# Two transformer blocks with an expert layer of gathered rows: the order of the first norm's turns, of the first expert sums and of the last gathers

## The chip, the core and the metric

The kernel is one program in Bass on one core of a Trainium2 chip: TensorE (PE) for matmuls, VectorE (DVE), ScalarE (ACT), GpSimd (POOL) and SyncE (SP), each with its own instruction queue, and 16 DMA engines that all queues share. The metric is the device time of one execution in microseconds, the median of several runs; less is better.

## What is computed

Batch 1, 256 tokens, model width 1024, float32. The second block ends with the part that takes half of the time.

```python
x = first_block(...)     # HGRN2 + pooling mixer, layer norm, squared-ReLU MLP of width 4096, layer norm
# second_block:
x = x + mixer(rmsnorm(x, norm_mix_g))          # MoBA attention, spatial gating MLP, two gates
x = x + memory_cross_attention(rmsnorm(x, norm_xa_g), rmsnorm(mem, norm_mem_g), w_q, w_kv, w_o)
x = x + peer_ffn(rmsnorm(x, norm_ffn_g), w_q, subkeys, w_down, w_up)
return rmsnorm(x, final_g)

def token_chunk(xc):                            # peer_ffn, for 128 tokens
    q = (xc @ w_q).reshape(128, 8, 2, 128)
    s = einsum("thpd,hpnd->thpn", q, subkeys)   # 8 heads, two lists of 128 scores
    s1, i1 = top_k(s[:, :, 0], 16)
    s2, i2 = top_k(s[:, :, 1], 16)
    top_s, top_pos = top_k(s1[..., :, None] + s2[..., None, :], 16)   # of 256 sums
    e = take(i1[..., :, None] * 128 + i2[..., None, :], top_pos)      # 16 of 16384 experts
    g = softmax(top_s)
    a = gelu(einsum("td,thkd->thk", xc, w_down[e]))
    return einsum("thk,thkd->td", g * a, w_up[e])
```

Each token and head reads 16 rows of w_down and 16 of w_up from HBM, 268 MB in all.

## The kernel before

**Weights.** The matmuls up to the cross attention run in a split form: ScalarE makes a high part of a weight block and VectorE the rest ("w_hi", "w_lo"), and PE multiplies three of the four products. SP loads a block of 1 MB into one of four buffers as soon as PE is done with the block four before. `take` waits for the split halves, `across` (line 646) multiplies in the transposed form, `to_across` (line 810) turns rows into columns by transposes, four at a time into one PSUM bank ("batch").

**First norm.** After the block "wo", VectorE normalizes XR in two column halves and signals `ln_z` twice. PE runs the first half of block "xka" (keys of the memory), then in `turn_first` the four batches "ln1T" 0 to 3 of four transposes each, then the second half of "xka". Of each two batches VectorE scales one into LT[:, 0] (line 2313) and ScalarE the other into LT[:, 1] (line 1501); ScalarE then copies both into the high part of both_C (line 1407) and VectorE subtracts for the low part (line 1908), after which the first "up" block (lines 691 and 694) may run its half. LT has one set of buffers: the second pair waits for the first's low part. Between its two pairs ScalarE copies "xka" out to KX (line 1384).

**Expert layer.** The 16 turns `it` are head `it % 8` of tokens 0 to 127 (turns 0 to 7) and 128 to 255 (8 to 15). For each of the 16 picks of a turn POOL issues one indirect DMA (line 3006) that gathers, for each of 128 tokens, one row of 8 KB, "down" and "up" side by side, into one buffer R. Number n = 16 it + k takes a buffer from `OPENED` (free after some earlier stage) or that of gather `USED_BY[n]`, once PE has counted its sums in `up_done`; POOL issues in strict order and waits for `idx_ready` where a new index is needed. Two picks form a pair g: VectorE's `dot_rows` (line 2783) takes the dot with the token, ScalarE the gelu, VectorE's `coefs` (line 2792) the product with the softmax weight, ScalarE two diagonal matrices DIAG (line 1802), and PE's `sums` (line 1278) adds DIAG times the "up" half into two PSUM banks, four matmul instructions a pick. Each engine's order over the turns is written out by hand.

In turn 0 the first index is ready ahead of the next seven and these ahead of the last eight (`first_eight`, `second_eight`, `decode_eight`: a position in the list of sums is split into two numbers, each looked up by comparing with iota, multiplying and adding up). Turn 0 is mixed with the cross attention of tokens 128 to 255: `cross_max` (VectorE), `cross_exps` (ScalarE, line 1713), `cross_weights` (VectorE, line 2564), `cross_turn` (PE, line 1177), `cross_turned` (ScalarE), `cross_values` (PE, line 1188) and `cross_out_second` (line 1209). `warm` loads ScalarE's table for another function.

**End.** The last pick (n = 255) has no diagonal: VectorE adds coef times its "up" row to the PSUM sums into XR, in two halves (line 2960), and the final norm and three stores follow.

## Time and profile before

| | |
|---|---|
| median of 3 runs | 1291.82 us (1291.52 to 1292.28) |
| profiled execution: its own time | 1292.65 us |
| its span, first to last instruction | 1290.9 us |
| busy: PE, DVE, ACT, POOL | 1178.1, 928.0, 555.2, 298.0 us |
| DMA: moved, mean rate | 396.14 MB, 307 GB/s |
| gathers | 256, 268.45 MB, 50.3% of 16 engines' span |
| mean granted TensorE clock | 0.990 |

How to read it: an engine's busy time is summed over stages with different limits, and PE's is modelled from pipelined starts. The profile gives time by instruction group, by stretch, and as a chain of releasers followed back from the last instruction. The numbers below are from that one profiled execution.

### The profile page before, as it was taken

Reading aid. Unit: us, or ns where it says so; the run is one execution under the profiler, and the core shown is the slowest. Engines: PE = TensorE matmul, PEld = TensorE weight load, DVE = VectorE, ACT = ScalarE, POOL = GpSimd, SP = SyncE. Lnnn points to the kernel's source line nnn. Section 1 sums busy time; section 2 is a strip of 40 time slices with the busy share of each in tenths; the row PEclk is TensorE's granted clock in tenths of the full one; section 3 lists DMA queues with packets and bytes.
Section 4 is the critical chain, followed back from the end, with each engine's and each line's share of the span. In section 5 each row is a group of like instructions: output and inputs, shape, how many; then the busy total and the mean of one; then the engine's idle time right before and its main releaser. Section 6 shows DMA issues by size and latency. Waiting matters only on the chain.

```text
span 1290.9 us, 16341 instructions
## 1 busy us (share of the span) xinstructions
PE 1178.1 (91%) x5734; PEld 829.1 (64%) x5734; DVE 928.0 (72%) x1854; ACT 555.2 (43%) x1014; POOL 298.0 (23%) x261
## 2 busy tenths in 40 slices
PE   9999999999999999999999989988987877777776
PEld 9988999888888899998855544544532323332322
DVE  6886758788854785587688786777677777777655
ACT  5833655466533547656435333332332222222312
POOL 0000000000000000000244555444554444545420
PEclk9999999999999999999999999999999999999999
DMA  7544455455555653466899999999999999999996
GB/s 290 189 170 144 164 210 208 160 191 195 210 213 192 201 194 135 166 245 238 345 400 421 418 420 419 420 419 420 420 419 420 420 420 419 422 418 422 418 421 256
DMA packets 55924, 396.14 MB, mean 307 GB/s; under 512 B 6320, under 2 KB 6320, under 8 KB 8752
## 3 DMA queue, kind: packets, MB, share of 16 engines
q0 software_dynamic: 36864, 268.45, 50.3%
q1 hardware_dynamic: 17136, 119.17, 25.6%
q10 hardware_dynamic: 1856, 7.60, 1.7%
q8 instruction: 44, 0.72, 0.2%
q14 instruction: 24, 0.20, 0.0%
HBM read 394.15 MB, written 1.05 MB: 306 GB/s over the span
## 4 chain that ended last, share of the span: by engine, by line
PE 60%; DMA 30%; DVE 5%; ACT 2%; issue 2%; POOL 1%; DVEq 0%; POOLq 0%; ACTq 0%
DMA R<-experts,IDX 30%; PE ps L646 12%; PE ps L1278 10%; PE ps L774 10%; PE ps L691 9%; PE ps L694 5%; PE ps L715 3%; PE ps L728 2%; PE ps L658 2%; PE ps L1106 2%; DVE R L2783 1%; ACT DIAG L1802 1%; POOL R L3006 1%; PE ps L1156 1%; PE ps L810 1%
## 5 line engine op out<-in xcount | busy, mean ns | idle before, releaser
L1278 PE MATMUL ps<-R,DIAG 128*128 128x512 f32 x1020 | 476.0, 612 | 97.3 <-ACT DIAG L1802 96.8
L1278 PEld LDWEIGHTS ps<-R,DIAG 128*128 128x128 f32 x1020 | 187.7, 193 | 358.0 <-issue 192.2
L3006 POOL DMA_INDIRECT R<-experts,IDX x256 | 296.7, 1159 | 513.3 <-PE ps L1278 281.7
L2783 DVE CUSTOM_DVE_ANT_0 R<-R,XN 128x1024 f32<-128x1024 f32 x256 | 312.9, 1227 | 132.8 <-DMA R<-experts,IDX 130.9
L1938 DVE TENSOR_TENSOR w_lo<-raw,w_hi 128x1024 fp32r<-128x1024 f32 x192 | 227.5, 1220 | 70.8 <-ACT w_hi L1335 66.7
L1335 ACT ACTIVATE w_hi<-raw 128x1024 fp32r<-128x1024 f32 x191 | 192.9, 1052 | 69.0 <-DMA raw<-weights 67.9
L1790 ACT ACTIVATE act_d<-dots,rst 128x2 f32<-128x2 f32 (+1 forms) x130 | 38.4, 296 | 305.3 <-DVE dots L2783 305.2
L1802 ACT ACTIVATE DIAG<-con,coef 128x128 f32<-128x128 f32 x255 | 88.6, 394 | 121.3 <-DVE coef L2792 119.0
L691 PE MATMUL ps<-both_C,w_hi 128*128 128x512 f32 x384 | 134.4, 394 | 1.3 <-DVE both_C L1908 1.3
L694 PE MATMUL ps<-both_C,w_lo 128*128 128x256 f32 x384 | 107.6, 280 | 0.0
L2984 POOL TENSOR_SCALAR_AFFINE_SELECT WS<-WS 128x1024 f32<-128x1024 f32 x1 | 1.1, 1090 | 437.7 <-DMA BS<-gbs 437.7
L691 PEld LDWEIGHTS ps<-both_C,w_hi 128*128 128x128 f32 x384 | 71.9, 187 | 18.1 <-issue 1.8
L694 PEld LDWEIGHTS ps<-both_C,w_lo 128*128 128x128 f32 x384 | 72.6, 189 | 0.0
L646 PE MATMUL ps<-both_A,w_hi 128*128 128x256 f32 x384 | 69.9, 284 | 0.2 <-issue 0.2
L646 PEld LDWEIGHTS ps<-both_A,w_hi 128*128 128x128 f32 x384 | 60.1, 192 | 0.6 <-issue 0.6
L646 PE MATMUL ps<-both_C,w_hi 128*128 128x256 f32 x320 | 58.8, 284 | 0.3 <-ACT GA L1384 0.3
L646 PE MATMUL ps<-both_A,w_lo 128*128 128x256 f32 x192 | 54.3, 283 | 0.0
L646 PEld LDWEIGHTS ps<-both_C,w_hi 128*128 128x128 f32 x320 | 50.2, 192 | 1.2 <-issue 0.7
L774 PE MATMUL ps<-w_hi,HT_hi 128*128 128x512 f32 x128 | 49.8, 389 | 0.0
L774 PE MATMUL ps<-w_lo,HT_hi 128*128 128x512 f32 x128 | 49.8, 389 | 0.0
L774 PE MATMUL ps<-w_hi,HT_lo 128*128 128x512 f32 x128 | 49.8, 389 | 0.0
L646 PE MATMUL ps<-both_C,w_lo 128*128 128x256 f32 x160 | 45.3, 283 | 0.0
(431 smaller groups left out, 1767.5 us busy)
## 6 DMA issues: line engine op xcount, KB each, us to landing
raw<-weights SPq DMA_DIRECT2D x95, 1024.0 KB, 4.8
PQW<-weights SPq DMA_DIRECT2D x8, 1024.0 KB, 7.1
R<-experts,IDX POOLq DMA_INDIRECT x256
raw<-weights SPq DMA_DIRECT2D x4, 512.0 KB, 8.6
LNR<-rows ACTq DMA_DIRECT2D x2, 1024.0 KB, 4.7
early_raw<-weights SPq DMA_DIRECT2D x2, 1024.0 KB, 6.9
XQ<-weights SPq DMA_DIRECT2D x2, 1024.0 KB, 6.6
XO<-weights SPq DMA_DIRECT2D x2, 1024.0 KB, 8.7
```

Source lines behind the costliest of these rows:

```text
L646: mm = pe.matmul(dst[:, c * T:(c + 1) * T], a[:, i, c * P:(c + 1) * P], b[:, k0 + i, :], start=(first and c == 0 and i == ks[0] and n == 0 ...
L691: pe.matmul(dst[:, c, :], w[0][:, k, c * P:(c + 1) * P], both[:, k, :, :].rearrange("p a b -> p (a b)"), start=(k == 0), stop=False, skip_ ...
L694: mm = pe.matmul(dst[:, c, 0:T], w[1][:, k, c * P:(c + 1) * P], both[:, k, 0, :], start=False, stop=(k == 7), skip_group_check=True)
L715: mm = pe.matmul(bank(r), o[:, 4 * k + i, m * P:(m + 1) * P], a[:, 2 * i:2 * i + 2, :].rearrange("p a b -> p (a b)"), start=(k == 0 and i ...
L774: mm = pe.matmul(psum[:, 4 + 2 * g + m, :], o[:, 4 * k + i, m * P:(m + 1) * P], a[:, 2 * i:2 * i + 2, :].rearrange("p a b -> p (a b)"), st ...
L1278: mm = pe.matmul(psum[:, 4 + 2 * m + n, :], DIAG[:, k, :], rows_[:, D + n * 512:D + (n + 1) * 512], start=(it % 8 == 0 and k == 0), stop=True,
L1335: act.activation(w_hi[s][:, 4 * h:4 * h + 4, :], raw[s][:, 4 * h:4 * h + 4, :], ACT.Copy).then_inc(hi_ready, 1)
L1790: act.activation(act_d[:, par, k0:k1], dots[:, par, k0:k1], ACT.Gelu_apprx_tanh, scale=rst[:, it // 8:it // 8 + 1]).then_inc(gelu_done, 1)
L1802: ins = act.activation(DIAG[:, k, :], ident, ACT.Copy, scale=coef[:, par, k:k + 1])
L1938: dve.tensor_tensor(w_lo[w][:, ks, :], raw[w][:, ks, :], w_hi[w][:, ks, :], ALU.subtract).then_inc(lo_ready, 1)
L2783: dve.tensor_tensor_reduce(out=rows_[:, 0:D], in0=rows_[:, 0:D], in1=XN[:, m, :], scale=1.0, scalar=0.0, op0=ALU.mult, op1=ALU.add, accum_ ...
L3006: pool.indirect_dma_start(out=R[u][:, :], out_offset=None, in_=experts, in_offset=bass.IndirectOffsetOnAxis(ap=IDX[:, it, k:k + 1], axis=0 ...
```

## The change

Four edits, and some semaphores joined.

1. First norm's turns: the second half of "xka" is cut into four parts of six matmuls, and the turns 0 and 1 come behind the first, the turns 2 and 3 behind the third. ScalarE copies "xka" out behind both LT pairs.
2. Turn 0: PE's sums of pair 1 come ahead of the softmax weights' turns of the second tokens, each later pair of the turn one place earlier. VectorE takes coefs of pairs 0 and 1 as early as their dots, and the cross attention's maxima, the second eight's decoding and `top_a` behind them; ScalarE does pair 1 ahead of the exponents. The buffers of two earlier stages enter the rotation at gathers 13 and 16 in place of 11 and 14.
3. `decode_eight` handles both sides of the position in one instruction where it had two.
4. The gathers 254 and 255 become four of 128 rows of 4 KB each: both "down" halves, then both "up" halves, with indices of their own, computed ahead of turn 14. PE waits for the "up" half of 254 and VectorE for that of 255.

```diff
-                  4: (24, ("xo_a", 3)), 5: (1, ("xq_b", 1)), 6: (2, ("xq_b", 1)), 11: (8, ("values", 1)),
-                  14: (14, ("xo_b", 1)), 21: (15, ("xo_b", 2))}
+                  4: (24, ("xo_a", 3)), 5: (1, ("xq_b", 1)), 6: (2, ("xq_b", 1)), 13: (8, ("values", 1)),
+                  16: (14, ("xo_b", 1)), 21: (15, ("xo_b", 2))}
...
# SP
-            wait_row(sp, 15, 15)
+            sp.wait_ge(last_up[1], 16)
...
# PE
-            def turn_first():
-                pe.wait_ge(ln_z, 1)
-                for j in range(2):
+            def turns(n):
+
+                pe.wait_ge(ln_z, n + 1)
+                for j in (2 * n, 2 * n + 1):
                     to_across("ln1T", XR, j)
-                pe.wait_ge(ln_z, 2)
-                for j in range(2, 4):
-                    to_across("ln1T", XR, j)
-
-            one("xka", 0, opB, across, mid=turn_first)
+
+            b, dst = BLOCK["xka"], bank(RING["xka"])
+            free_bank(RING["xka"])
+            w = take(b % 4, half_end(b, 0))
+            across(dst, w, opB, range(4), last=False).then_inc(gemm_done, 1)
+            w = take(b % 4, half_end(b, 1))
+            across(dst, w, opB, (4, 5), first=False, last=False, cs=(0,))
+            turns(0)
+            across(dst, w, opB, (6, 7), first=False, cs=(0,))
+            across(dst, w, opB, (4, 5), first=False, last=False, cs=(1,))
+            turns(1)
+            across(dst, w, opB, (6, 7), first=False, cs=(1,)).then_inc(gemm_done, 1)
...
                     rows_ = wait_row(pe, it, k)
+                    if (it, k) == (15, TOPK - 2):
+                        pe.wait_ge(last_up[0], 16)
...
+                        if (it, k, n) == (15, TOPK - 2, 0):
+                            mm.then_inc(last_sum, 1)
...
             sums(0, 0)
+            sums(0, 1)
             cross_turn(1, 0)
             cross_turn(1, 1)
-            sums(0, 1)
+            sums(0, 2)
             cross_values(1)
-            sums(0, 2)
+            sums(0, 3)
             wait_aux(pe, "xpvb")
             cross_out_second(0)
-            sums(0, 3)
+            sums(0, 4)
             query(2, 0)
-            sums(0, 4)
+            sums(0, 5)
             head_scores(2, 0)
-            sums(0, 5)
             cross_out_second(1)
...
# ScalarE
-                if j == 1:
-                    evac("xka", 0, KX[:, 0:2, :], ACT.Copy, further=False)
-                else:
-                    ahead(BLOCK["up"] + 2)
+            evac("xka", 0, KX[:, 0:2, :], ACT.Copy, further=False)
+            ahead(BLOCK["up"] + 2)
...
             diagonals(0, 0)
+            activate(0, 1)
             warm(ACT.Exp)
             cross_exps(1, 0)
             cross_exps(1, 1)
             warm(ACT.Gelu_apprx_tanh)
             head_scores(1, 0)
-            activate(0, 1)
+            activate(0, 2)
             cross_turned(1, 0)
             cross_turned(1, 1)
-            activate(0, 2)
+            activate(0, 3)
             values_second()
-            activate(0, 3)
...
# VectorE, decode_eight
-                for q in range(2):
-                    st.do(dve.tensor_tensor(
-                        eq0[:, q, ks, 0:side],
...
+                both, picked = [P, 2, ks.stop - ks.start, side], eq0[:, :, ks, 0:side]
+                st.then(dve.tensor_tensor(
+                    picked, C("iota")[:, 0:side].rearrange("p (q a b) -> p q a b", q=1, a=1).broadcast_to(both),
+                    cpf[:, :, ks].rearrange("p q (a b) -> p q a b", b=1).broadcast_to(both), ALU.is_equal))
+                st.then(dve.tensor_tensor(
+                    picked, picked, tif[:, :, 0:side].rearrange("p q (a b) -> p q a b", a=1).broadcast_to(both),
+                    ALU.mult))
+                st.then(dve.tensor_reduce(ef[:, :, ks], picked, AX, ALU.add))
...
             dot_rows(0, 0)
             top_h(0)
+            dot_rows(0, 1, ks=(2,))
             coefs(0, 0)
-            decode_eight(high8, 16)
+            dot_rows(0, 1, ks=(3,))
+            coefs(0, 1)
             cross_max(1, 0)
             cross_max(1, 1)
-            dot_rows(0, 1)
+            dot_rows(0, 2, ks=(4,))
+            decode_eight(high8, 16)
+            dot_rows(0, 2, ks=(5,))
             cross_weights(1, 0)
+            coefs(0, 2)
             cross_weights(1, 1)
-            coefs(0, 1)
             top_a(1)
-            dot_rows(0, 2)
-            coefs(0, 2)
-            top_b(1)
             dot_rows(0, 3)
             coefs(0, 3)
+            top_b(1)
...
+            st.then(dve.scalar_tensor_tensor(out=last_index, in0=ef[:, 0, 14:16], scalar=float(NK),
+                                             in1=ef[:, 1, 14:16], op0=ALU.mult, op1=ALU.add))
+            dve.tensor_scalar(last_rows[:, 0:2], last_index, 2.0, None, ALU.mult).then_inc(idx_ready, 1)
+            dve.tensor_scalar(last_rows[:, 2:4], last_index, 2.0, 1.0, ALU.mult, ALU.add).then_inc(idx_ready, 1)
...
-            dve.wait_ge(up_done, 255)
...
+            dve.wait_ge(last_up[1], 16)
             for n, cs in enumerate(halves_):
+                dve.wait_ge(*((up_done, 255) if n else (last_sum, 1)))
...
# POOL, gathers
+                    if n >= 16 * TOPK - 2:
+                        continue
...
+            pool.wait_ge(idx_ready, 20)
+            for h in range(2):
+                for n in (16 * TOPK - 2, 16 * TOPK - 1):
+                    u, c = UNIT_OF[n], 2 * h + n % 2
+                    pool.indirect_dma_start(
+                        out=R[u][:, h * D:h * D + D], out_offset=None,
+                        in_=experts.rearrange("e (h d) -> (e h) d", h=2),
+                        in_offset=bass.IndirectOffsetOnAxis(ap=last_rows[:, c:c + 1], axis=0)
+                    ).then_inc(last_up[n % 2] if h else row_in[u], 16)
```

The joined semaphores: lb_diff and lb_exp become one (`lb_turn`), gv_ms and gv_sd another (`gv_turn`), each waited for at 1 and 2.

## Rows read from the trace of the kernel before

**Rows 1.** The page, part 4: the chain that ended last, shares by engine.
```profile
PE 60%; DMA 30%; DVE 5%; ACT 2%; issue 2%; POOL 1%; DVEq 0%; POOLq 0%; ACTq 0%
```

**Rows 2.** Stretches: length, busy us (instructions) by engine, PE clock, DMA share, GB/s.
```profile
253.00:632.00 379.00, 376.80 (x2338) 333.69 (x2339) 262.60 (x327) 211.83 (x318) 2.18 (x2) 1.00 0.57 203
632.00:645.00 13.00, 13.00 (x101) 11.99 (x100) 11.14 (x48) 5.21 (x11) 6.90 (x6) 1.00 0.97 359
645.00:655.00 10.00, 7.20 (x18) 3.06 (x17) 9.43 (x30) 7.01 (x19) 2.65 (x3) 0.83 1.01 420
655.00:665.00 10.00, 10.00 (x36) 5.40 (x35) 8.56 (x27) 1.85 (x6) 4.93 (x5) 1.00 0.95 352
665.00:718.50 53.50, 52.66 (x206) 30.03 (x205) 40.62 (x109) 24.54 (x61) 24.74 (x21) 1.00 1.01 420
1270.00:1280.00 10.00, 8.71 (x21) 3.67 (x20) 5.46 (x12) 2.38 (x7) 0.00 (x0) 1.00 0.59 244
```

**Rows 3.** Timelines 244 to 254 us, and one stretch (245.9 to 249.1) of line 646 alone.
```profile
244.19 2.00 PE L810 MATMUL ps<-con,XR 128*128 128x128 f32 x16 [0.64 <-DVE XR L2288]
...
245.90:249.10 3.20, 3.11 (x24) 2.93 (x24) 1.00 0.00 0
...
247.11 1.29 DVE L1908 TENSOR_TENSOR both_C<-LT,both_C 128x512 fp32r<-128x512 f32 x2 [1.03 <-ACT both_C L1407]
...
248.32 0.99 DVE L2313 TENSOR_SCALAR LT<-ps,vec 128x256 f32<-128x256 f32 x2
...
249.10 0.60 ACT L1384 ACTIVATE KX<-ps 128x512 f32<-128x512 f32 x1 [1.57 <-PE ps L646]
...
249.59 1.02 ACT L1501 ACTIVATE LT<-ps,vec 128x256 f32<-128x256 f32 x2
...
253.21 0.47 PE L691 MATMUL ps<-both_C,w_hi 128*128 128x512 f32 x1 [1.31 <-DVE both_C L1908]
```

**Rows 4.** VectorE's timeline: decoding of the list positions.
```profile
632.57 0.35 DVE L2716 TENSOR_REDUCE ef<-eq 128x8 f32<-128x64 f32 x2
...
644.01 0.48 DVE L2716 TENSOR_REDUCE ef<-eq 128x8 f32<-128x128 f32 x2
...
667.17 0.69 DVE L2695 TENSOR_REDUCE ef<-eq 128x32 f32<-128x512 f32 x1
```

**Rows 5.** Timelines of POOL, PE and VectorE, 630 to 656 us.
```profile
630.48 1.09 POOL L3006 DMA_INDIRECT R<-experts,IDX  x1 [191.16 <-DVE IDX L2742]
...
647.81 1.69 POOL L3006 DMA_INDIRECT R<-experts,IDX  x1 [1.28 <-PE ps L1278]
...
654.99 0.94 POOL L3006 DMA_INDIRECT R<-experts,IDX  x1 [5.49 <-PE ps L1278]
...
643.43 3.60 PE L1278 MATMUL ps<-R,DIAG 128*128 128x512 f32 x8
...
649.55 1.46 PE L1177 MATMUL ps<-con,XS 128*128 128x128 f32 x8 [2.52 <-DVE XS L2564]
...
651.15 5.40 PE L1278 MATMUL ps<-R,DIAG 128*128 128x512 f32 x8
...
642.10 0.16 DVE L2792 TENSOR_TENSOR coef<-act_d,GW 128x2 f32<-128x2 f32 x1 [1.30 <-ACT act_d L1790]
```

**Rows 6.** Line 3006 alone, 630 to 718.6 us: durations in ns, first and last start.
```profile
L3006 POOL DMA_INDIRECT R<-experts,IDX x36: 939/942/1942, 630.5 to 718.5; - x36
```

**Rows 7.** VectorE's timeline, 1279 to 1284 us.
```profile
1279.33 1.23 DVE L2783 CUSTOM_DVE_ANT_0 R<-R,XN 128x1024 f32<-128x1024 f32 x1 [0.73 <-DMA R<-experts,IDX]
...
1281.83 1.23 DVE L2783 CUSTOM_DVE_ANT_0 R<-R,XN 128x1024 f32<-128x1024 f32 x1 [0.73 <-DMA R<-experts,IDX]
...
1283.69 1.41 DVE L2960 SCALAR_TENSOR_TENSOR XR<-R,coef,ps 128x512 f32<-128x512 f32 x2
```

**Rows 8.** Stretches: the load of MEM, and the last stores.
```profile
144.00:145.00 1.00, 1.00 (x11) 1.00 (x10) 1.00 (x2) 0.00 (x0) 0.00 (x0) 1.00 1.01 418
1288.50:1289.50 1.00, 0.00 (x0) 0.00 (x0) 0.00 (x0) 0.00 (x0) 0.00 (x0) 0.50 0.93 350
```

More of the change, by code:

```diff
@@ L356, in build @@
         lb = small("lb", [P, 8])
+        last_index, last_rows = lb[:, 0:2], lb[:, 4:8].bitcast(U32)
         lbx = small("lbx", [P, 8])
@@ L430, in build @@
         dve_step, act_step, pool_step = sem("dve_step"), sem("act_step"), sem("pool_step")
-        lb_diff, lb_exp = sem("lb_diff"), sem("lb_exp")
+        lb_turn = sem("lb_turn")
         f_ready, logf_ready, g_ready = sem("f_ready"), sem("logf_ready"), sem("g_ready")
@@ L446, in build @@
         att_max, att_exp, att_p, att_t = sem("att_max"), sem("att_exp"), sem("att_p"), sem("att_t")
-        gv_sq, gv_ms, gv_sd, gv_n, ws_masked, gm_ready = (
-            sem("gv_sq"), sem("gv_ms"), sem("gv_sd"), sem("gv_n"), sem("ws_masked"), sem("gm_ready"))
+        gv_sq, gv_turn, gv_n, ws_masked, gm_ready = (
+            sem("gv_sq"), sem("gv_turn"), sem("gv_n"), sem("ws_masked"), sem("gm_ready"))
         m2_ready = sem("m2_ready")
@@ L464, in build @@
         top_v, top_e, idx_ready = sem("top_v"), sem("top_e"), sem("idx_ready")
+        last_sum = sem("last_sum")
+        last_up = [sem(f"last_up{n}") for n in range(2)]
         row_in = {u: sem(f"row_in{u}") for u in R}
@@ L639, in parts, with across @@
                 return ((w[0], op[1]), (w[1], op[0]), (w[0], op[0]))
-            def across(dst, w, op, ks, first=True, last=True, k0=0):
-                for c in range(2):
+            def across(dst, w, op, ks, first=True, last=True, k0=0, cs=(0, 1)):
+                for c in cs:
                     for i in ks:
@@ L1420, in hi_turned @@
                 ins.then_inc(split_hi, 1)
-            act.wait_ge(lb_diff, 1)
-            act.activation(lbd[:, :], lbd[:, :], ACT.Exp).then_inc(lb_exp, 1)
+            act.wait_ge(lb_turn, 1)
+            act.activation(lbd[:, :], lbd[:, :], ACT.Exp).then_inc(lb_turn, 1)
             ahead(2)
@@ L1617, in _ @@
             ins.then_inc(gv_sq, 1)
-            act.wait_ge(gv_ms, 1)
-            act.activation(ssq[:, :, 2], ssq[:, :, 2], ACT.Sqrt).then_inc(gv_sd, 1)
+            act.wait_ge(gv_turn, 1)
+            act.activation(ssq[:, :, 2], ssq[:, :, 2], ACT.Sqrt).then_inc(gv_turn, 1)
             for j in range(2):
@@ L1976, in _ @@
             st.do(dve.tensor_tensor(lbd[:, 0:8], l0, lbx[:, :], ALU.subtract))
-            dve.tensor_tensor(lbd[:, 8:16], l1, lbx[:, :], ALU.subtract).then_inc(lb_diff, 1)
-            dve.wait_ge(lb_exp, 1)
+            dve.tensor_tensor(lbd[:, 8:16], l1, lbx[:, :], ALU.subtract).then_inc(lb_turn, 1)
+            dve.wait_ge(lb_turn, 2)
             st.then(dve.tensor_tensor(lb[:, :], lbd[:, 0:8], lbd[:, 8:16], ALU.add))
@@ L2423, in _ @@
             dve.tensor_scalar(ssq[:, :, 2], ssq[:, :, 1], 1.0 / 512, RMS_EPS, ALU.mult, ALU.add
-                              ).then_inc(gv_ms, 1)
-            dve.wait_ge(gv_sd, 1)
+                              ).then_inc(gv_turn, 1)
+            dve.wait_ge(gv_turn, 2)
             st.then(dve.reciprocal(ssq[:, :, 3], ssq[:, :, 2]))
@@ L2703, in decode_eight @@
                 st.then(dve.tensor_copy(cpf[:, :, ks], cp[:, :, ks]))
-                for q in range(2):
-                    st.do(dve.tensor_tensor(
-                        eq0[:, q, ks, 0:side],
-                        C("iota")[:, 0:side].rearrange("p (a b) -> p a b", a=1).broadcast_to(shape),
-                        cpf[:, q, ks].rearrange("p (a b) -> p a b", b=1).broadcast_to(shape), ALU.is_equal))
-                st.sync()
-                for q in range(2):
-                    st.do(dve.tensor_tensor(
-                        eq0[:, q, ks, 0:side], eq0[:, q, ks, 0:side],
-                        tif[:, q, 0:side].rearrange("p (a b) -> p a b", a=1).broadcast_to(shape), ALU.mult))
-                st.sync()
-                for q in range(2):
-                    st.do(dve.tensor_reduce(ef[:, q, ks], eq0[:, q, ks, 0:side], AX, ALU.add))
-                st.sync()
+                both, picked = [P, 2, ks.stop - ks.start, side], eq0[:, :, ks, 0:side]
[6 more added lines that the diff above has]
+                st.then(dve.tensor_reduce(ef[:, :, ks], picked, AX, ALU.add))
                 index(0, listed or ks)
@@ L2776, in top_h, with dot_rows @@
                 st.then(dve.tensor_scalar(row_of(GW, it), gx[:, :], gs[:, 1:2], None, ALU.mult))
-            def dot_rows(it, g):
+            def dot_rows(it, g, ks=None):
                 m, par = half_and_column(it)
-                for k in range(*picks(it, g)):
+                for k in ks or range(*picks(it, g)):
                     rows_ = wait_row(dve, it, k)
```

## The prediction

> **What bounds the kernel now.** I read the page first, then the rates by stretch, then the timelines of the four places that the change touches. The page's chain that ended last has TensorE (PE) for 60% and the gathers for 30% [rows 1]. The reader is to see two regimes. From 253 to 632 us PE is busy 376.80 of 379 us and the DMA share is 0.57 [rows 2]: what delays PE there delays the end. From 665 us the gathers run at 420 GB/s [rows 2]. A gather is 128 rows of 8 KB, 1.0486 MB, so one takes 2.50 us, and the dots of the last two start 2.50 us apart [rows 7]. There the end moves only if the stream starts earlier, has fewer holes, or leaves less behind its last byte. The holes are early: 655 to 665 us ran at 352 GB/s [rows 2], a loss of 10 x 68/420 = 1.6 us. In 1270 to 1280 us the share falls to 0.59 while rows still come every 2.5 us [rows 2, 7]: some engines are done, one or more lag, and these set the end. Behind the last landing (1281.8) stand 9.1 us to the span's end, 1290.9.
>
> **First norm's turns (a gain of 1.1).** Before, PE turns all 16 blocks at 244.19, in 1.8 us, and then does half 1 of "xka", 24 matmuls in about 3 us, 0.12 each; ScalarE copies KX from it at 249.10, and only behind that, at 249.59, begins the last LT pair [rows 3]. The new order puts six of the matmuls (0.7 us) into PE's idle 0.64 before 244.19. Turns 0 and 1 then end at 245.1 as before, 12 matmuls at 246.6, turns 2 and 3 at 247.5, the last six at 248.2. VectorE's next use of those turns is at 248.32 [rows 3], so that their being later is covered by 0.8 us. ScalarE, no longer held by KX, waits only for VectorE's both_C pair (247.11 + 1.29 = 248.4) and starts LT at 248.5, 1.1 earlier. The chain behind it, 3.6 us from there to PE at 253.21, where PE had idled 1.31 [rows 3], waits for nothing else. KX now lies behind it, in time in which PE works, and its bank is wanted a block (5 us) later; uncovered it would cost its 0.5. SP's loads wait for PE's own progress and move along. PE is full from there to 632 [rows 2], so the 1.1 arrives at the first gather. Ends: 0.7, what PE itself gains at the end of xka (248.9 to 248.2), and 1.3, its idle time.
>
> **Both index sides at once (a gain of 0.1).** Three pairs of VectorE instructions become three single ones. A pair of 128x64 takes 0.35 us, a pair of 128x128 0.48, a single 128x512 0.69 [rows 4]. The pairs rise by 1.0 ns an element of both, so a single of 256 is about 0.69 - 0.26 = 0.43 and one of 128 about 0.3: 3 x 0.05 = 0.15 us for gathers 2 to 8 and as much for the second eight. The second gather's bytes follow the first's with little queued; I take 0.1, ends 0 and 0.2. Joining the semaphores of lb and gv keeps every wait: nothing, either way.
>
> **Second pair's sums first (a gain of 0.5 after what it gives back).** Before, PE idles 2.52 us for the softmax weights, turns them, and then takes 5.40 us instead of 3.60 for pair 1's sums [rows 5]; the granted clock over the stretch is 0.83, so part of it ran at the lower level, 1.2 GHz, right after the idle time [rows 2]. Buffers come free late, and POOL issues the tenth gather at 654.99, after 5.49 us. Up to 655 us 13 x 359 + 10 x 420 = 8.87 MB came [rows 2], 8.5 of nine gathers; the ninth ends at about 656.4. By an estimate from that, new bytes need at least 1.5 us from their issue (at 630.48 the first; nothing before 632 fits the rate), so the tenth's begin at 656.8. That is the hole.
> Now after the change, in the same clock. The third row's bytes are in at 632 + 3.15/0.359 = 640.8 and usable about 1 us later; its dot ends at 643.1, and coefs of pair 0 go from 642.10 to 643.2 or a little less: PE's sums, 643.43 before, start at 644.3. The fourth row's dot ends at 645.8, DIAG of pair 1 at 647.1; its sums follow without a gap, 647.8 to 651.2. ScalarE's Exp table, four exponents, Gelu table and scores take it to 653. VectorE decodes the second eight behind the fifth row's dot, 649.3 to 651.7, and POOL's ninth gather waits for just that index: 651.7 instead of 647.81 [rows 5]. The tenth and eleventh follow at 652.9 and 654.2, their buffers being free since 649.5 and 651.2; then 658.2, 660.8, 662.6. The eighth's bytes end at 653.9 and the ninth's begin at 653.3 at best: no room, but no hole. Every later one is issued 1.2 us or more before it must be. So most of the 1.6 us goes, and short queues keep some; I take 0.9, ends 0 and 1.6. PE still idles, 651.2 to 653.7, for the same softmax, and I let the slower clock follow again (1.8 us); if it doesn't, PE is that much earlier.
> What it gives back: PE's later sums come 0.8 us later in this frame, and the queue reaches them 1.0 us earlier (0.9 + 0.1). By 718.5 us 8.87 + 3.52 + 22.47 = 34.86 MB are in [rows 2], 33.2 gathers, and the 36th is issued [rows 6]: its turn is 1.76 x 2.5 = 4.4 us away; less 1.8 for its start that is a room of 2.6, which shrinks to 0.8. I let small holes take 0.4 there: net 0.5, ends -0.8 and 1.5.
>
> **Last two gathers as half rows (a gain of 1.65).** The bytes stay the same; both rows' "down" halves come first, the "up" halves last. T is the last landing. Before, from T to the first XR instruction it is 1283.69 - 1281.83 = 1.86 us, for dot, gelu and coef [rows 7]. Now halves land at T - 3.75, - 2.5, - 1.25 and T. The first row's dot, gelu and coef last from -3.75 to -2.0, the second's behind them from -1.95 to -0.1. So XR's first half starts at T + 0.05, 1.8 earlier. PE's four matmuls of the first row, 0.43 each (3.60 for eight, [rows 5]), start at T - 1.2: two are done at -0.3, four at +0.6, and XR's second half, wanted at +0.8, hardly waits; 0.05 for that. VectorE's three small index instructions (0.5 us) lie ahead of turn 14, where it idles about 0.7 us before each dot [rows 7]; POOL's two added issues, under 2 us, lie 25 us ahead of their bytes. SP's first store waits for T, as before. 4 KB pieces: the load of MEM has them and ran at 418 GB/s, as 8 KB ones do; the last stores' 2 KB pieces ran at 350 [rows 8], which bounds the four halves' loss at 5.0 x (420/350 - 1) = 1.0 us. I charge 0.1. Ends 0.8 and 1.9.
> Here a rule speaks against the change. The Trainium skill, "DMA: Bandwidth & Descriptors", section "Anatomy of one DMA — SWDGE (gpsimd) path", gives every such DMA 2.0 us fixed plus its bytes at 436 GB/s. By that page, an estimate, four halves take 4 x 3.2 instead of 2 x 4.4 us, 4.0 us more, if nothing overlapped. The trace doesn't agree for queued gathers: they come every 2.50 us.
>
> **Sum.** 1.1 + 0.1 + 0.5 + 1.65 = 3.35 us. The profiled execution took 1292.65, 1290.9 in the span and 1.75 around it; it is 0.83 above the median of the runs shown. 1292.65 - 3.35 - 0.83 = 1288.5 us.
>
> **Rivals.**
> (a) The later sums bound the stream. If the queue can't live with less than its room of 2.6 us at 718, PE's supply of buffers counts, 0.8 later in its frame, and hole and index give nothing: 1.1 - 0.8 + 1.65 = 1.95, so 1289.9. For it: no stretch shows a full rate with less room. Against: half the room is left. Chance 0.2.
> (b) The hole closes wholly and the room suffices: 1.1 + 0.2 + 1.6 + 1.7 = 4.6, so 1287.2. For it: 420 GB/s wherever two gathers are queued. Chance 0.12.
> (c) Half rows don't act: each of the two added gathers costs a start of 1.7 us (first issue to first bytes) though queued. 3.35 - 3.4: 1291.9, no change. Against: the pace of 2.50. Chance 0.05.
> (d) Slower: the lagging engine is paced by packets, not bytes. If a 4 KB packet takes it as long as one of 8 KB, four halves take 10.0 us and not 5.0. The tail still gains 1.86: 1.7 + 1.86 - 5.0 = -1.4, so 1293.3. It decides from 2.1 us a half. Against: 418 GB/s in 4 KB pieces; for it: those were not gathered. Chance 0.05.
> The forecast has 0.58, for 1287.6 to 1289.7.
>
> **How the numbers follow.** A measurement tells 0.2%, 2.6 us, from no change: faster is below 1289.2. The forecast is that but for 0.07, (b) wholly, (a) for 0.03: 0.66. Slower is above 1294.4, beyond (d): 0.04. The rest, 0.30, is the same. The range takes in (b) and (a) with the spread of their terms: 1286.6 to 1290.8.
>
> **What would show it.** In the profile after: the last LT pair about 1.1 earlier, and PE's second half of the first "up" block at about 252.1; in that shifted clock POOL's ninth gather some 4 us later but the tenth 2 earlier; 655 to 665 us well above 352 GB/s, and whether a stretch before 725 fell below 418; XR's first half within 0.2 us of the last landing. It is wrong if "up" doesn't start earlier, if the ninth gather's index comes after 653 us (a hole of its own), or if the last half rows take over 1.5 us each.

## The result, and the profile after

The changed kernel takes 1294.4 us at the median of 22 runs (1292.03 to 1297.54), the kernel before 1292.11 us in 22 runs beside them. The ratio is 1.0014, with an interval of 1.0009 to 1.002: 1.8 us slower by the ratio (the medians lie 2.3 apart), within the 0.2% that I had called no change, and outside the forecast of 1288.5 (1286.6 to 1290.8). The profiled execution took 1294.63 us, 1292.9 of them in the span.

Line numbers moved: the pairs' matmuls are line 1291 (1278 before), the dots 2790 (2783), coefs 2799 (2792), the gathers 3023 (3006), XR 2975 (2960), LT on ScalarE 1516 (1501), KX 1399 (1384), the two matmul lines of "up" 694 and 697 (691 and 694), softmax weights 2577 (2564), DIAG 1815 (1802).

ScalarE's and TensorE's timelines around the first norm, after, beside [rows 3]:
```profile
248.38 1.02 ACT L1516 ACTIVATE LT<-ps,vec 128x256 f32<-128x256 f32 x2 [0.98 <-DVE both_C L1921]
...
250.49 0.58 ACT L1399 ACTIVATE KX<-ps 128x512 f32<-128x512 f32 x1
...
251.99 0.47 PE L694 MATMUL ps<-both_C,w_hi 128*128 128x512 f32 x1 [0.51 <-DVE both_C L1921]
```
LT starts 1.21 us earlier, KX stands behind it, and the second half of the first "up" block starts 1.22 earlier. The first gather is issued at 629.37 instead of 630.48: the 1.1 us arrived.

The stretches after, columns as in [rows 2]:
```profile
632.00:645.00 13.00, 11.82 (x90) 10.76 (x89) 9.58 (x32) 3.83 (x9) 6.44 (x6) 1.00 0.99 382
645.00:655.00 10.00, 7.90 (x24) 3.72 (x23) 9.22 (x30) 8.73 (x21) 4.41 (x4) 0.96 0.96 374
655.00:665.00 10.00, 10.00 (x33) 5.25 (x32) 9.04 (x32) 1.88 (x5) 4.58 (x6) 0.87 0.99 378
665.00:700.00 35.00, 30.36 (x98) 15.51 (x98) 25.15 (x72) 12.45 (x31) 12.62 (x13) 0.95 1.01 419
700.00:718.50 18.50, 18.50 (x86) 11.52 (x85) 13.55 (x35) 10.91 (x28) 6.89 (x8) 1.00 0.97 369
718.50:740.00 21.50, 21.50 (x78) 11.75 (x77) 16.38 (x48) 6.29 (x17) 10.29 (x10) 1.00 0.97 379
1270.00:1280.00 10.00, 7.41 (x17) 2.87 (x16) 5.42 (x12) 2.67 (x8) 0.00 (x0) 1.00 0.94 385
```
The old hole has only changed its shape: 374 and 378 GB/s in the two stretches that had 420 and 352. And there is a new and larger one, 700 to 740 us at 369 and 379 GB/s, where the kernel before ran at 420. It costs (18.5 x 51 + 21.5 x 41)/420 = 4.3 us. TensorE is busy all through it; it had been idle before it, in 665 to 700 us, where 30.36 of 35 us are busy.

TensorE's timeline after, the rows with idle time ahead of them (in brackets, with what ended it), and the last picks:
```profile
643.65 7.13 PE L1291 MATMUL ps<-R,DIAG 128*128 128x512 f32 x16 [1.18 <-ACT DIAG L1815]
...
652.65 0.66 PE L1188 MATMUL ps<-con,XS 128*128 128x128 f32 x4 [1.86 <-DVE XS L2577]
...
654.04 5.29 PE L1291 MATMUL ps<-R,DIAG 128*128 128x512 f32 x8
...
676.57 3.70 PE L1291 MATMUL ps<-R,DIAG 128*128 128x512 f32 x8 [1.58 <-ACT DIAG L1815]
...
694.07 5.40 PE L1291 MATMUL ps<-R,DIAG 128*128 128x512 f32 x8 [3.06 <-ACT DIAG L1815]
...
1277.45 8.85 PE L1291 MATMUL ps<-R,DIAG 128*128 128x512 f32 x20 [1.29 <-ACT DIAG L1815]
```
The two waits at 676.57, ahead of sums(0, 5), and at 694.07, ahead of sums(1, 0), are new; before, TensorE idled there for 0 and 0.84 us. Who was late is read on the two engines in front of it, ScalarE and VectorE:
```profile
675.03 0.38 ACT L1823 ACTIVATE QP<-ps 128x256 f32<-128x256 f32 x1 [9.27 <-PE ps L731]
675.31 0.29 ACT L1803 ACTIVATE act_d<-dots,rst 128x2 f32<-128x2 f32 x1
...
675.62 0.16 DVE L2799 TENSOR_TENSOR coef<-act_d,GW 128x2 f32<-128x2 f32 x1 [5.19 <-ACT act_d L1803]
...
680.81 0.47 ACT L1790 ACTIVATE SC<-ps,rst 128x256 f32<-128x256 f32 x1 [4.29 <-PE ps L759]
...
682.11 0.16 DVE L2799 TENSOR_TENSOR coef<-act_d,GW 128x2 f32<-128x2 f32 x1 [3.31 <-ACT act_d L1803]
```
The same places in the kernel before, with TensorE's sums(1, 0):
```profile
672.24 0.38 ACT L1810 ACTIVATE QP<-ps 128x256 f32<-128x256 f32 x1 [6.38 <-PE ps L728]
...
672.84 0.16 DVE L2792 TENSOR_TENSOR coef<-act_d,GW 128x2 f32<-128x2 f32 x1 [2.49 <-ACT act_d L1790]
...
690.66 3.70 PE L1278 MATMUL ps<-R,DIAG 128*128 128x512 f32 x8 [0.84 <-ACT DIAG L1802]
```
In the changed kernel ScalarE stands 9.27 us (6.38 before) ahead of queries(2, 0), the copy of what TensorE's query(2, 0) (line 731) computes. Pair 5's gelu stands behind that copy and starts at 675.31, though pair 5's dots were done at 670.4; VectorE waits 5.19 us (2.49 before) for it. Then ScalarE waits 4.29 us for head_scores(2, 0) (line 759), with pair 6's gelu behind it, and VectorE another 3.31. Everything behind those coefs, the residual and the first dots of turn 1 among it, comes late, and so does DIAG for sums(1, 0).

Why the early stretch isn't better: VectorE stands at the dots of rows 2 and 3 until they land, with the softmax and the second eight indices behind them.
```profile
641.57 1.23 DVE L2790 CUSTOM_DVE_ANT_0 R<-R,XN 128x1024 f32<-128x1024 f32 x1 [2.08 <-DMA R<-experts,IDX]
...
643.96 1.23 DVE L2790 CUSTOM_DVE_ANT_0 R<-R,XN 128x1024 f32<-128x1024 f32 x1 [1.08 <-DMA R<-experts,IDX]
...
650.48 0.17 DVE L2703 SCALAR_TENSOR_TENSOR IDX<-ef 128x8 uint32<-128x8 f32 x1
...
650.92 1.68 POOL L3023 DMA_INDIRECT R<-experts,IDX  x1 [4.07 <-PE ps L1291]
...
652.90 1.39 POOL L3023 DMA_INDIRECT R<-experts,IDX  x1 [0.31 <-issue]
```
3.2 us of VectorE are lost there; the index of the ninth gather is written at 650.48 to 650.65, and POOL issues it 0.3 us later (the profile names TensorE, but the buffer waits for pick 1's sums only, which end near 647.2). The tenth follows at 652.90, 23.5 us behind the first issue instead of 24.5 [rows 5].

The end of the stream after: SP's first store, which waits for the last landing, and XR.
```profile
1285.03 0.34 SPq L626 DMA_DIRECT2D out<-YO  x1
...
1285.59 1.50 DVE L2975 SCALAR_TENSOR_TENSOR XR<-R,coef,ps 128x512 f32<-128x512 f32 x2 [0.60 <-PE ps L1291]
```
XR starts 0.56 us behind the last landing; before it was 1.86 [rows 7]. From that store to the span's end it is 7.87 us, before 9.03. But VectorE waits 0.60 for the sums: TensorE's last 20 matmuls, from pair (10, 11) on, run without a gap for 8.85 us.

### The profile page after: what moved, and what is told of

The parts are those of the page before. It is cut to its first block, busy times and chain, and to the rows that moved or that the text cites. A ratio compares the mean times of both kernels' runs of the same rounds, so it can differ in the third digit from the quotient of the medians.

```text
span 1292.9 us, 16340 instructions
## 1 busy us (share of the span) xinstructions
PE 1180.7 (91%) x5734; PEld 830.5 (64%) x5734; DVE 927.4 (72%) x1851; ACT 555.8 (43%) x1014; POOL 295.0 (23%) x263
## 4 chain that ended last, share of the span: by engine, by line
PE 61%; DMA 29%; DVE 4%; ACT 2%; issue 2%; POOL 1%; DVEq 0%; ACTq 0%
DMA R<-experts,IDX 29%; PE ps L649 12%; PE ps L1291 11%; PE ps L777 10%; PE ps L694 9%; PE ps L697 5%; PE ps L731 3%; PE ps L718 3%; PE ps L661 2%; PE ps L1117 2%; DVE R L2790 1%; POOL R L3023 1%; ACT DIAG L1815 1%; PE ps L813 1%; PE ps L824 1%
## 5 line engine op out<-in xcount | busy, mean ns | idle before, releaser
L3023 POOL DMA_INDIRECT R<-experts,IDX x254 | 289.6, 1140 | 521.2 <-PE ps L1291 282.7
L697 PE MATMUL ps<-both_C,w_lo 128*128 128x256 f32 x384 | 107.6, 280 | 0.0
L2799 DVE TENSOR_TENSOR coef<-act_d,GW 128x2 f32<-128x2 f32 (+1 forms) x130 | 21.2, 163 | 37.0 <-ACT act_d L1803 26.0
```

The source lines that it names most:

```text
L697: mm = pe.matmul(dst[:, c, 0:T], w[1][:, k, c * P:(c + 1) * P], both[:, k, 0, :], start=False, stop=(k == 7), skip_group_check=True)
L3023: pool.indirect_dma_start(out=R[u][:, :], out_offset=None, in_=experts, in_offset=bass.IndirectOffsetOnAxis(ap=IDX[:, it, k:k + 1], axis=0 ...
```

## The experiments

Three numbers are read from each kernel's trace: the first gather's issue; the stream, from there to SP's first store (which waits for the last landing in every kernel here); and the rest to the span's end. "Waits" are TensorE's idle us ahead of sums(0, 5) and sums(1, 0). Ratios are to runs of the kernel before on the same chip, with 95% intervals.

```
kernel                    ratio   interval         issue   stream  rest  waits
before                    1                        630.48  651.39  9.03  0    0.84
changed                   1.0014  1.0009 - 1.0020  629.37  655.66  7.87  1.58 3.06
e1 turns alone            0.9997  0.9988 - 1.0006  629.75  650.04  9.01  0    0.84
e2 order alone            1.0039  1.0026 - 1.0052  630.84  654.00  9.06  1.58 3.07
e3 half rows alone        0.9993  0.9984 - 1.0001  631.28  650.19  7.93  0    0.84
e4 changed, old order     0.9980  0.9971 - 0.9988  629.83  650.52  7.85  0    0.84
e5 ScalarE moved          1.0003  0.9994 - 1.0012  631.38  652.01  7.91  0    3.07
e6 VectorE filled         1.0020  1.0010 - 1.0031  629.60  653.87  7.83  1.58 3.06
e7 both                   1.0003  0.9991 - 1.0015  630.87  655.24  7.89  0    3.07
e8 e4, split pair         0.9985  0.9976 - 0.9994  629.96  651.50  7.44  0    0.84
e9 query back             0.9996  0.9987 - 1.0005  631.14  651.10  7.86  0    0.84
e10 e9, VectorE filled    0.9988  0.9979 - 0.9997  630.00  650.24  7.86  0    0.84
e11 e10, split pair       0.9980  0.9970 - 0.9989  631.30  650.95  7.45  0    0.84
e12 query late alone      1.0028  1.0018 - 1.0037  632.45  654.84  9.01  1.58 3.07
e13 order repaired alone  1.0     0.9991 - 1.0009  632.35  650.29  9.06  0    0.84
```

**The parts one by one (e1 to e4).** e1 is the kernel before with `turns(n)` and ScalarE's KX behind LT; e2 with the second pair's order and OPENED; e3 with the half rows; e4 is the changed kernel with the old order. Of e4's edit TensorE's first lines:
```
-            sums(0, 1)
             cross_turn(1, 0)
             cross_turn(1, 1)
+            sums(0, 1)
+            cross_values(1)
             sums(0, 2)
...
```

> The kernel before with the first norm's new turn order alone (no other part of the change). Theory (the loss lies in the second pair's order): this part pays in full, 1.1 us less than before, since the stream of gathers simply starts 1.1 us earlier and no hole is added; the DMA rate over 655 to 725 us stays at its values of before. Rival (an earlier start of the stream is itself lost, because the queue overtakes TensorE's supply of buffers before 725 us): 0 to 0.3 us less than before, with a rate below 415 GB/s somewhere between 700 and 735 us.

> The kernel before with the second pair's order alone: pair 1's sums ahead of the second tokens' softmax and every later pair one place earlier, with the buffers' order that goes with it. Theory: this part alone costs 4 us or more (last landing +3.2 in the changed kernel in spite of 1.3 us of earlier start), so 1296 to 1297 beside 1292.1, with the holes of the changed kernel: below 400 GB/s in 704 to 732 us, TensorE idle for some 3 us ahead of sums (1,0). Rival (the loss comes from the half rows or only from all parts together): within 1 us of the time before, and no such holes.

> The kernel before with the last two gathers as half rows alone (and the joined semaphores and the three small index instructions that go with it). Theory: 1.2 us less than before: from the last landing to the span's end 7.9 instead of 9.1 us, the landing itself where it was. Rival (4 KB pieces of a gather, or two more gathers, cost the stream time): 0 to 2 us more than before, with the last landing 1 to 3 us later.

> The changed kernel with the second pair's order put back as before (turns, both index sides at once and half rows stay). Theory: the parts add up, 1.1 + 0.2 + 1.2 = 2.5 us less than before, about 1289.6, so 4.8 us less than the changed kernel. Rival (the parts get in each other's way: an earlier stream start is lost in a shallow queue): 1.0 to 1.5 us less than before, about 1290.9.

The order alone costs 0.39%, 5.0 us (five executions; 3.4 to 6.7 by the interval), with a stream 2.6 us longer than that of the kernel before and 4.0 longer than e1's. Without it, the rest of the change gives 0.20%, 2.6 us: e4 took 1289.91 us at the median of its 12 executions (one of them took 2377.68 us and is not in the ratio) beside 1292.46. So the loss lies in the order, and the other parts add up to the 2.5 us that was expected of e4. Singly they are too small for this measurement (e1's interval is -1.6 to +0.8 us, e3's -2.1 to +0.1); the traces show each. The rival to e1, an earlier start that is lost later, is not seen: its stretches from 655 to 740 us run at 418 to 420 GB/s. e2's trace has the changed kernel's two waits, and its stretches 700 to 718.5 and 718.5 to 740:
```profile
700.00:718.50 18.50, 18.50 (x88) 11.78 (x88) 13.52 (x36) 11.40 (x30) 7.09 (x7) 1.00 0.99 395
718.50:740.00 21.50, 21.50 (x78) 11.81 (x77) 17.42 (x51) 6.71 (x18) 9.97 (x9) 1.00 0.98 383
```

**Which of three engines is late (e5 to e7).** e5 moves one ScalarE call, e6 fills VectorE's idle time, e7 does both:
```
 (ScalarE, e5)                     (VectorE, e6)
-            queries(2, 0)         -            dot_rows(0, 1, ks=(2,))
             activate(0, 5)                     coefs(0, 0)
+            queries(2, 0)         -            dot_rows(0, 1, ks=(3,))
                                   +            decode_eight(high8, 16)
                                   +            dot_rows(0, 1)
                                                coefs(0, 1)
                                                cross_max(1, 0), cross_max(1, 1)
                                   -            dot_rows(0, 2, ks=(4,)), decode_eight(high8, 16)
                                   -            dot_rows(0, 2, ks=(5,))
                                   +            dot_rows(0, 2)
```

> The changed kernel, with ScalarE's activate(0, 5) (gelu and DIAG of pair 5) ahead of queries(2, 0) instead of behind it. In the changed kernel queries(2, 0) waits on ScalarE for TensorE's query(2, 0), 9.3 us idle, while pair 5's dots are long done; TensorE then waits 1.58 us for pair 5's DIAG and 3.06 us for that of turn 1's pair 0, and works the next pair at the lower clock (5.40 for 3.60 us). Theory 1 (ScalarE's order is what makes the late hole): the 1.58 goes to 0, the 3.06 to under 1.5, the stretch 704 to 732 us comes back to 410 GB/s or more, and the time falls by 2.5 to 4 us, to 1290.5 to 1292. Theory 2 (the late hole comes from VectorE, behind since its waits for rows at 641 to 645 us, so that the same idle time of TensorE only turns up elsewhere): less than 1 us.

> The changed kernel, with VectorE's coefs(0, 0) and the decoding of the second eight indices ahead of the dots of pair 1, where VectorE waits 2.08 and 1.08 us for rows 2 and 3 in the changed kernel; then the dots of pair 1, coefs(0, 1), the softmax's maxima, the dots of pair 2. TensorE's and ScalarE's orders stay. Theory 2 (VectorE's idle 3.2 us is the root): the ninth gather's issue goes from 20.3 us after the last of the first seven's start to about 3 us earlier, the softmax weights come about 3 us earlier, the hole at 652 to 660 us goes and most of the late one as well, and the time falls by 3 to 4.5 us. Theory 1 (ScalarE's order makes the late hole): only the early hole goes, 1.5 to 2 us less, and the stretch 704 to 732 us stays below 395 GB/s.

> The changed kernel with both of these moves. Theories 1 and 2 alike give some 4 to 5 us less than the changed kernel, 1289.5 to 1290.5, level with the kernel that has the second pair's old order; if TensorE's new order itself costs (cross_out and the query ahead of pairs that were early before), it stays above that by over 1 us, and holes are left between 700 and 735 us with TensorE never idle.

Neither theory held whole. In e5 the wait ahead of sums(0, 5) is gone, and so is the late hole, as theory 1 had it; but the wait ahead of sums(1, 0) stays, 3.07 us, and the ratio is only 0.11% below the changed kernel's, 1.4 us, with intervals that overlap. Its trace, ScalarE, VectorE, TensorE and the two stretches:
```profile
679.88 0.47 ACT L1790 ACTIVATE SC<-ps,rst 128x256 f32<-128x256 f32 x1 [3.56 <-PE ps L759]
...
681.18 0.16 DVE L2799 TENSOR_TENSOR coef<-act_d,GW 128x2 f32<-128x2 f32 x1 [4.82 <-ACT act_d L1803]
...
693.15 3.70 PE L1291 MATMUL ps<-R,DIAG 128*128 128x512 f32 x8 [3.07 <-ACT DIAG L1815]
...
700.00:718.50 18.50, 18.50 (x86) 11.56 (x85) 14.82 (x36) 10.69 (x30) 9.16 (x7) 1.00 1.01 419
718.50:740.00 21.50, 21.50 (x81) 11.94 (x81) 17.37 (x49) 7.67 (x18) 11.65 (x10) 1.00 1.01 419
```
The stall has moved one pair on, from queries to head_scores(2, 0), which TensorE has only behind sums(0, 5). In e6 the early hole is closed and the late one stays, 350 GB/s in 700 to 718.5 us, and the time is not better than the changed kernel's (on e5's chip it is 0.17% above e5):
```profile
645.00:655.00 10.00, 6.46 (x21) 2.78 (x20) 7.59 (x22) 8.36 (x21) 4.68 (x4) 1.00 1.01 420
655.00:665.00 10.00, 10.00 (x37) 5.46 (x36) 9.30 (x31) 1.94 (x6) 5.34 (x5) 1.00 1.01 419
...
700.00:718.50 18.50, 18.50 (x77) 10.83 (x76) 14.68 (x36) 10.47 (x29) 8.56 (x7) 1.00 0.97 350
```
e7 spread from 1289.58 to 1296.65 us, with a median of 1292.41; its profiled execution has the wait of 3.07 again and works at the lower clock behind two waits (granted clock 0.83 in 655 to 665 us and 0.71 in 690 to 700), with 329 GB/s in 700 to 718.5 us.

The wait of 3.07 us alone does not make the late hole. In e5 the eight matmuls behind it took 3.70 us, and there is none. In the changed kernel, e2, e6 and e12 they took 5.38 to 5.40, in e7 6.73, and these five have it, though four of them have the wait of 1.58 as well. No run separates the wait from the clock behind it.

What e5 and e6 leave over is TensorE's own order: the change put query(2, 0) and head_scores(2, 0), too, one pair later, since each pair of sums went ahead of what stood before it.

**The query put back (e9 to e11, e8).** e9 is the changed kernel with
```
             cross_out_second(0)
-            sums(0, 4)
             query(2, 0)
-            sums(0, 5)
+            sums(0, 4)
             head_scores(2, 0)
+            sums(0, 5)
             cross_out_second(1)
```
so that only pairs 1 to 3 are earlier. e10 adds e6's VectorE order, and e11 and e8 (which is e4 with it) the split of a pair:
```
-        PICKS = [PAIRS] * 15 + [PAIRS[:6] + [(12, 13), (13, 14), (14, 15), (15, 16)]]
+        PICKS = [PAIRS] * 15 + [PAIRS[:5] + [(10, 11), (11, 12), (12, 13), (13, 14), (14, 15), (15, 16)]]
```

> The changed kernel, with query(2, 0) and head_scores(2, 0) on TensorE one pair earlier: sums(0, 3), cross_out(0), query(2, 0), sums(0, 4), head_scores(2, 0), sums(0, 5), cross_out(1). So pairs 1 to 3 keep their new place ahead of the softmax, the turn and the values, and from the query on TensorE's order is that of before; ScalarE and VectorE stay as changed. Theory 3 (what costs is that the change put the query and its head scores behind one more pair on TensorE, and that ScalarE and VectorE, which take their instructions in order, hold pair 5's and 6's gelu, coefs and DIAG behind them): the waits of 1.58 and 3.06 us of TensorE go to 0 and about 0.8, VectorE's wait of 5 us for a coef too, the stretch 704 to 732 us comes back to at least 415 GB/s, and the time falls by 3 us or more, to 1291.4 or less. Rival (VectorE has simply more to do ahead of these pairs, so that the idle time turns up elsewhere): less than 1.5 us.

> The same, and VectorE's coefs(0, 0) and the decoding of the second eight ahead of pair 1's dots. Theory 3: with the late hole gone by the query's old place, this takes the early one (ninth and tenth gather, 652 to 660 us) as well: 1.0 to 1.8 us less than with the query moved back alone, level with the kernel that has the old order of the second pair, 1289.5 to 1290.5. Rival (the early hole is covered: the slowest DMA engine catches up in it): no difference to the query moved back alone.

> The same, and in turn 15 rows 10 and 11 as two single picks. In the earlier run the split cut the time from the last landing to the end from 7.9 to 7.4 us. If that is a gain of its own it shows beside the kernel without it on the same chip: 0.3 to 0.6 us less. Rival: no difference, since the spread of the stream's end is as large.

> The changed kernel with the second pair's order of before (the best so far, 1289.9), and in turn 15 rows 10 and 11 as two single picks instead of one pair. With half rows TensorE's last 20 matmuls run without a gap for 8.85 us from pair (10, 11)'s DIAG on and end 0.6 us after VectorE wants the sums. Theory (that backlog bounds the end): row 10's sums start 2.3 us earlier, VectorE's wait of 0.62 us for the sums falls to under 0.1, and the time from the last landing to the span's end from 7.9 to 7.3: 0.5 to 0.6 us less. Rival (the last half row's landing or the clock bounds it: TensorE idles between the single rows and falls to the lower clock): no gain, or up to 1 us more.

The traces of e9, ScalarE's and VectorE's timeline and the two stretches: both of TensorE's waits are as in the kernel before, VectorE's longest wait for a coef in 640 to 740 us falls from 5.2 to 1.4, and the late hole is gone:
```profile
671.59 0.38 ACT L1823 ACTIVATE QP<-ps 128x256 f32<-128x256 f32 x1 [4.14 <-PE ps L731]
...
672.27 0.16 DVE L2799 TENSOR_TENSOR coef<-act_d,GW 128x2 f32<-128x2 f32 x1 [0.36 <-ACT act_d L1803]
```
```profile
700.00:718.50 18.50, 18.50 (x82) 11.28 (x81) 12.90 (x31) 8.16 (x24) 6.95 (x7) 1.00 1.01 419
718.50:740.00 21.50, 21.49 (x77) 11.55 (x77) 18.03 (x53) 7.58 (x18) 11.48 (x11) 1.00 1.01 420
```
The stream is 4.6 us shorter than the changed kernel's, the ratio (on another chip) 0.18% lower, 2.3 us, somewhat less than the 3 I had expected, with intervals that do not overlap. e10's ratio is another 0.08% lower, 1.0 us, at the low end of what was expected, but the two intervals overlap; its stream is 0.9 us shorter than e9's.

The split shortens the rest by 0.41 us in both kernels that have it (7.85 to 7.44, 7.86 to 7.45), and XR no longer waits for the sums; 0.5 to 0.6 was expected. Times can't show it: e11 is 0.08% below e10, e8 0.05% above e4 (on another chip), all within their intervals.

**The step alone, both ways (e12, e13).** e12 is the kernel before with query(2, 0) behind sums(0, 4) and head_scores(2, 0) behind sums(0, 5), nothing else; e13 is e2 with the query put back and VectorE filled.

> The kernel before with one thing changed: query(2, 0) and head_scores(2, 0) stand one pair later on TensorE, behind sums(0, 4) and sums(0, 5), as they do in the changed kernel; pair 1, the softmax and the other engines stay as before. Theory 3 (this placing is the costly piece of the change): the waits of the changed kernel appear here too, TensorE idle about 1.6 us ahead of sums(0, 5) and some 3 us ahead of sums(1, 0), VectorE some 5 us ahead of a coef, holes after 704 us, and the time rises by 2 to 4 us over before. Rival (it costs only together with the moved first pairs, which leave TensorE late): within 1 us of before.

> The kernel before with the second pair's order alone, but with the query and its head scores where they were and VectorE's decoding of the second eight ahead of pair 1's dots. It measures by itself what my sum had put at 0.5 us of gain. Theory 3: 0 to 1.5 us less than before, the stream from first issue to last landing 650.2 us beside 651.3 in the kernel before, 1 us less where the softmax comes late, nothing less where it does not (650.0 to 650.5 in the two executions of the old order without a hole). Rival (the order has a price of its own beyond the query): 1 us or more above before.

e12 reproduces most of the loss in the kernel before: 0.28%, 3.6 us (2.3 to 4.8 by the interval), with the same two waits, the same stall on ScalarE and a hole to 317 GB/s. Its timelines of ScalarE and TensorE, and the stretch:
```profile
676.87 0.38 ACT L1810 ACTIVATE QP<-ps 128x256 f32<-128x256 f32 x1 [9.54 <-PE ps L728]
...
682.66 0.47 ACT L1777 ACTIVATE SC<-ps,rst 128x256 f32<-128x256 f32 x1 [4.29 <-PE ps L756]
...
695.93 5.40 PE L1278 MATMUL ps<-R,DIAG 128*128 128x512 f32 x8 [3.07 <-ACT DIAG L1802]
```
```profile
700.00:718.50 18.50, 18.50 (x89) 11.83 (x88) 13.50 (x33) 12.42 (x30) 8.80 (x7) 1.00 0.88 317
```
e13, what is left of the order without that step, is level with the kernel before, 1.0 within 0.9991 to 1.0009, on the same chip as e12.

## Why the prediction was wrong, point by point

**What bounds the kernel.** Right: a hole in the stream before 740 us came out at the end, and so did an earlier start. One sentence of it I read too strongly. The hole of 655 to 665 us does not come with the old order. Three of the five other traces that have this order around 650 us, e1, e3 and e4, show no hole (e4's row, beside 352 in [rows 2]):
```profile
655.00:665.00 10.00, 10.00 (x26) 4.48 (x25) 8.93 (x27) 2.36 (x7) 5.54 (x5) 1.00 1.01 419
```
In these TensorE idles 1.3 to 1.4 us for the softmax weights, in the kernel before and e8 2.52 and 2.43 (352 and 333 GB/s). Of these two groups the first has streams of 650.0 to 650.5 us, the second 651.4 and 651.5. By these few traces the hole that I set out to close was worth 0.9 to 1.5 us, and in some of them only. e1, e3 and e4 ran on one chip, so that the difference may lie with the chip.

**First norm's turns.** Right: 1.1 forecast. LT's last pair starts at 248.26 to 248.85 us in the ten traces with the new order and at 249.59 to 249.79 in the five without, 1.2 on average. "Up" follows, and KX's place costs nothing that shows: from LT's last pair to the first gather it takes 380.9 us before and 381.0 in the changed kernel.

**Both index sides at once.** Right in kind: the single instruction of 256 takes 0.42 us and that of 128 0.29, where 0.43 and 0.3 were estimated; the second gather is issued 0.2 us sooner behind the first (632.08 less 629.37, before 633.39 less 630.48). It has no run of its own.

**Second pair's sums first: the step that failed.** I forecast a net gain of 0.5, ends -0.8 and 1.5; alone it cost 5.0 us (e2). The details around 650 us held: the ninth gather 4.2 us later against the first, the tenth earlier, though by 1.0 and not by 2. In this frame (the changed kernel's times plus 1.1 us) the ninth was issued 0.3 us later than forecast, and the tenth came 2.0 behind it (1.68 busy and 0.31) where I had 1.2. Pair 0's sums began 1.3 and not 0.8 us later. What failed is the sentence "PE's later sums come 0.8 us later in this frame". It followed TensorE's list as if only its own length counted. query(2, 0) and head_scores(2, 0) moved behind one more pair with it, and on ScalarE, which takes its instructions in order, their copies stand ahead of pair 5's and pair 6's gelu. So the coefs, DIAGs and sums of these pairs wait for a TensorE result that TensorE itself has put behind an earlier pair, and sums(1, 0) ends 8.7 us later than in e4 (699.5 and 690.8) where I had 0.8. That one placing alone costs 3.6 us beside the 5.0 of the whole order (e12, e2). What the other 1.4 is stays open, and it lies within the intervals: e10 is 1.0 us below e9, for VectorE's 3.2 idle us ahead of rows 2 and 3, but that difference is not clear of noise either. Repaired, the order gives nothing that these runs can tell from zero (e13), so that the forecast 0.5 is neither shown nor excluded.

**Last two gathers as half rows.** The mechanism held in the main, the size was too high: 1.65 forecast (0.8 to 1.9), 1.1 to 1.2 us in the rest to the span's end (e3, e4 and the changed kernel). I had let PE's matmuls of row 14 start at T - 1.2 as if TensorE were free then. It is behind: pair (10, 11) comes as a pair, its DIAG releases five rows' matmuls that run 8.85 us in one piece, and XR waits 0.6 for their end. e8 and e11, where the pair is split, get 0.41 of it back. The 4 KB pieces were priced at 0.1 with an end of 1.0: streams with them are 650.2 and 650.5 us, e1's without them 650.0, e13's 650.3: at most 0.5, and not told from nothing. Neither the extra start of each gather nor a pace by packets, which I had given 0.05 each, is seen.

**The sum.** With the measured terms: turns -1.1, index sides -0.2, half rows -1.15, order +5.0, together +2.5; measured +1.8, which the interval of the order's term (3.4 to 6.7) allows. My range took the order's end at a loss of 0.8, from one term alone, and no rival had ScalarE or VectorE late. Rival (a) came nearest in kind, late sums that bound the stream, but with the same 0.8 for them. That is why the range did not hold the time.

**A better version.** e4, the changed kernel without its order, beats both: 0.9980 of before (0.9971 to 0.9988), 1289.91 us. e11 stands at the same ratio with the repaired order and the split pair; no runs on one chip set the two against each other.

## What to carry to other kernels

When a call is moved past another in one engine's hand-written list, write down for every call that it passes who reads its result, and what stands behind that reader in its own engine's list: the price here came by way of a copy on ScalarE, and TensorE paid it 5 us behind the late query's start and 14 us behind that of the late head scores. Work put ahead of a wait for a landing should be what is ready; a dot placed ahead of ready work idles its engine for the whole wait. And before a hole in one trace is made the target, see whether other executions of the same code, on other chips too, have it.

## What the runs showed that I had not expected

**Two levels before the stream.** From LT's last pair (near 249 us) to the first gather's issue it takes 380.9 to 381.5 us in nine traces, and 382.6 to 382.8 in six (e5, e7, e9, e11, e12, e13), whatever the change; TensorE is busy and at full granted clock in both. In "up" a block takes 5.55 us in e4 and 5.65 in e5:
```profile
277.70 0.60 ACT L1533 ACTIVATE US<-ps 128x512 f32<-128x512 f32 x1 [1.77 <-PE ps L697]
283.25 0.60 ACT L1533 ACTIVATE US<-ps 128x512 f32<-128x512 f32 x1 [1.77 <-PE ps L697]
```
```profile
277.85 0.60 ACT L1533 ACTIVATE US<-ps 128x512 f32<-128x512 f32 x1 [1.87 <-PE ps L697]
283.51 0.60 ACT L1533 ACTIVATE US<-ps 128x512 f32<-128x512 f32 x1 [1.88 <-PE ps L697]
```
No row says why. Both levels occur on one chip (e5 and e6). The difference is as large as the terms that were forecast, and adds to the spread in which e1 and e3 are lost.

**A signal that comes 1.2 us late.** ScalarE's copy of the second tokens' query starts 0.26 us behind the next TensorE block in five traces (changed, e1 to e4) and 1.43 to 1.58 behind it in the other ten, the kernel before among them. GpSimd's gather that waits for the same matmuls is late with it, by 1.0 to 1.2 us. In the six traces with the old order around 650 us TensorE's wait for the softmax goes with it: 1.3 to 1.4 us where the copy is early, 2.4 to 2.5 where it is late. e1 to e4 ran on one chip and e5 to e13 on three others, so that it may go with the chip. What holds it back I can't say.

**The clock behind a wait.** Behind idle time of 3.06 to 3.07 us the eight matmuls took 5.38 to 5.40 us in the changed kernel, e2, e6 and e12, 6.73 in e7, and 3.70 in e5, with a granted clock over 690 to 700 us of 0.83 in the first four, 0.71 in e7 and 1.00 in e5; behind 2.4 to 2.5 us and the eight turns, 5.40 in the kernel before and in e8 and 4.53 in e12; behind 1.8 to 2.1 us, 5.29 in the changed kernel and 3.60 in e2, e5 and e9. The same wait can cost 3.0 us, 1.7 or nothing.

**The end of the stream.** In 1270 to 1280 us the DMA share is 0.59 before and 0.94 in the changed kernel, but its last landing is 3.2 us later. Over the ten microseconds from 11.9 to 1.9 ahead of the last landing it is 0.59 and 0.67: 0.67 to 0.74 in the five traces with a late hole, 0.53 to 0.61 in eight of the other ten, 0.64 in e9 and 0.67 in e11. That would fit engines that are behind and catch up in the holes, but no row here shows the single engines. By 732 us 36.9 gathers' bytes are in, 39.5 in e4 (by the rates in stretches of 4 us), 6.3 us behind; at the last landing, 1285.03 and 1280.35, it is only 4.7.
